# Hybrid decoder layer on one core: modulation blocks in pairs with three projections between their slots, and two half blocks beside q3

## What is computed

```python
mod = jnp.dot(jax.nn.silu(c), w_ada[l]) + b_ada[l]          # 6 vectors of 2048 for each of 9 sequences
sh1, sc1, g1, sh2, sc2, g2 = jnp.split(mod[:, None, :], N_MOD, axis=-1)
h = rmsnorm(x, g_mix[l]) * (1 + sc1) + sh1
z = jnp.dot(h, w_in[l])
zq, zk, zv, zu, gq, gk, gv, gg, ga = jnp.split(z, split_idx, axis=-1)
# window attention on q, k, v; causal pooling on u; gated linear attention (4 heads) on gq, gk, gv, gg, ga
x = x + g1 * jnp.dot(mix, w_out[l])
h2 = rmsnorm(x, g_ffn[l]) * (1 + sc2) + sh2
gate, up = jnp.split(jnp.dot(h2, w_gu[l]), 2, axis=-1)
x = x + g2 * jnp.dot(jax.nn.silu(gate) * up, w_down[l])
```

## Time and profile before

| | |
|---|---|
| median of three runs | 2444.57 us (2444.43 to 2444.83) |
| the profiled execution | 2438.74 us, its span 2436.6 us |
| TensorE busy | 2321.5 us (95%), mean granted clock 0.985 |
| VectorE, ScalarE, GpSimd busy | 1550.0, 922.1, 240.6 us |
| HBM read and written | 365.45 and 54.08 MB, 172 GB/s over the span |
| matmuls of the projections (L1948) | 4704 of 289 to 303 ns each |
| chain that ended last | PE 91%, DMA 3%, DVE 3%, issue 2%, ACT 1% |

### The profile page before, as it was taken

One profiled execution on the slowest core, in us unless ns is written; L12 is line 12 of the kernel. 1 busy time (PEld: TensorE's weight loads), 2 busy tenths in 40 slices (PEclk: granted clock), 3 DMA queues, 4 the chain that ended last, 5 costly groups with the idle time before them and its releaser, 6 DMA issues.

```text
span 2436.6 us, 44374 instructions
## 1 busy us (share of the span) xinstructions
PE 2321.5 (95%) x18645; PEld 2173.4 (89%) x18645; DVE 1550.0 (64%) x2240; ACT 922.1 (38%) x1328; POOL 240.6 (10%) x289
## 2 busy tenths in 40 slices
PE   5689999999999999899999999999999989999996
PEld 1179888888887899899999999999999989999996
DVE  0442642333324322887888888888788878888898
ACT  2122432323233222654444444444444433333443
POOL 3150240000000111100000000000000211011131
PEclk9989999999999999999999999999999999999998
DMA  9955465655563433223433443344344676365552
GB/s 340 345 184 184 155 168 176 226 166 204 176 212 107 173 114 115 109 102 137 169 129 121 159 166 137 137 169 141 124 160 152 260 271 226 132 217 191 181 216 87
DMA packets 191078, 422.43 MB, mean 173 GB/s; under 512 B 14692, under 2 KB 116884, under 8 KB 188832
## 3 DMA queue, kind: packets, MB, share of 16 engines
q1 hardware_dynamic: 171072, 341.35, 40.8%
q0 software_dynamic: 17216, 73.78, 8.6%
q10 hardware_dynamic: 2592, 4.46, 0.5%
HBM read 365.45 MB, written 54.08 MB: 172 GB/s over the span
## 4 chain that ended last, share of the span: by engine, by line
PE 91%; DMA 3%; DVE 3%; issue 2%; ACT 1%; POOL 0%; SPq 0%; DVEq 0%; POOLq 0%; ACTq 0%
PE PJ L2327 28%; PE PS L2327 28%; PE PJ L1948 25%; DMA AR<-in_weights 3%; PE PJ L1901 2%; PE PJ L2292 1%; PE PS L2183 1%; PE PJ L1891 1%; PE PS L2292 1%; PE PJ L2269 1%; PE PJ L1913 1%; DVE X L1868 0%; PE PS L2221 0%; PE PS L2186 0%; DVE HS L1790 0%
## 5 line engine op out<-in xcount | busy, mean ns | idle before, releaser
L2327 PE MATMUL PS<-HS,WO 128*128 128x272 f32 x5376 | 686.3, 289 | 10.8 <-issue 10.1
L2327 PEld LDWEIGHTS PS<-HS,WO 128*128 128x128 f32 x5376 | 681.4, 189 | 12.3 <-issue 12.3
L2327 PE MATMUL PJ<-HS,WO 128*128 128x272 f32 x5376 | 683.0, 289 | 0.0
L2327 PEld LDWEIGHTS PJ<-HS,WO 128*128 128x128 f32 x5376 | 679.7, 188 | 0.0
L1115 ACT ACTIVATE WO<-GR 128x1024 fp32r<-128x1024 f32 (+1 forms) x462 | 477.1, 1033 | 511.7 <-PE PS L2327 246.9
L1643 DVE TENSOR_TENSOR WO<-GR,WO 128x1024 fp32r<-128x1024 f32 (+1 forms) x462 | 555.7, 1203 | 120.4 <-ACT WO L1115 120.2
L1948 PE MATMUL PJ<-HH,WH 128*128 128x272 f32 x1568 | 347.0, 303 | 18.4 <-issue 8.0
L1948 PE MATMUL PJ<-HL,WH 128*128 128x272 f32 x1568 | 327.1, 290 | 0.0
L1948 PE MATMUL PJ<-HH,WL 128*128 128x272 f32 x1568 | 325.5, 289 | 0.0
L1274 DVE TENSOR_TENSOR WL<-RW,WH 128x1024 fp32r<-128x1024 f32 x102 | 130.8, 1286 | 281.5 <-ACT WH L854 281.2
L1948 PEld LDWEIGHTS PJ<-HH,WH 128*128 128x128 f32 x1568 | 247.5, 191 | 52.7 <-issue 41.0
(11 more groups left out here) (310 smaller groups left out, 1871.7 us busy)
## 6 DMA issues: line engine op xcount, KB each, us to landing
GR<-in_weights SPq DMA_DIRECT2D x264, 512.0 KB, 6.8
AR<-in_weights SPq DMA_DIRECT2D x256, 256.0 KB, 4.5
RW<-in_weights SPq DMA_DIRECT2D x102, 512.0 KB, 4.7
HS<-act_parts POOLq DMA_DIRECT2D x91, 544.0 KB, 5.9
act_parts<-SQ SPq DMA_DIRECT2D x40, 952.0 KB, 7.0
AR<-in_weights SPq DMA_DIRECT2D x64, 512.0 KB, 5.3
MIX<-in_xT SPq DMA_DIRECT2D x1, 4352.0 KB, 17.0
X<-in_xT POOLq DMA_DIRECT2D x4, 1088.0 KB, 9.8
```

What stands on the lines that cost most here:

```text
L2327: mm = e.matmul(out, w[part], HS[:, HS_AT[QUARTER[i]], y, (2 * first + k) % (KT // 2), :], start=OPENS[i] and k == 0 and x == 0, stop=k == ...
```

## The change

It does four things.

- The whole blocks are made in the order 0, 4, 1, 5, 2, 6, 3, 7 (`ADA_ORDER`), shift and scale of the same 512 features in turn. They use one pair of banks (`PS` 0 and 1) in place of two, so each block waits for the copy of the one before, and its turn stands behind slot 1 of the next block.
- k, v and q0 (`FIRST_TILES` = 3; q0 in `PS` 2 and 3) are issued by units, k by k: lots of three units stand behind every second slot of blocks 4 to 7 at the places `UNITS_AT`, ten lots for k = 0 to 9; k = 10 and 11 follow the last turn, and k = 12 to 15 come projection by projection. `project_two` isn't used there any more, and v's transposes stand beside q1.
- Tiles 0 to 2 are loaded ahead of block 3, tiles 3 to 5 ahead of block 5, tiles 6 to 8 behind the last slot. The sum over x moves from block 3 to block 2. VectorE's and ScalarE's orders follow.
- The half block that stood beside q0 moves on: q1 has the first, q2 the second, q3 the third and the fourth (behind units 3 and 11, turned behind 7 and 14). u0 and all behind it keep theirs. In SyncE's loop the half blocks start at q1's tile in place of q0's.

```diff
-ROWS = [V_W + n for n in range(4)] + [W_V[n] + x for n in W_TILES[2:] for x in range(2)]
+ROWS = [V_W, V_W + 1, W_V["q0"], V_W + 2, V_W + 3, W_V["q0"] + 1]
+ROWS += [W_V[n] + x for n in W_TILES[3:] for x in range(2)]
...
-SUM_AT = 3
-H_AT = 5
+SUM_AT = 2
+ADA_ORDER = (0, 4, 1, 5, 2, 6, 3, 7)
+FIRST_TILES = 3
+UNITS_AT = ((4, 5), (4, 7), (5, 1), (5, 3), (5, 5), (5, 7), (6, 1), (6, 3), (7, 3), (7, 5))
...
-            if n == ADA_V * (A_FIRST - 1):
-                for t in range(RAW):
-                    load(At(t))
+            if n in (ADA_V * 3, ADA_V * 5):
+                for t in range(FIRST_TILES):
+                    load(At(t + (FIRST_TILES if n > ADA_V * 3 else 0)))
             load_ada(n)
+        for t in range(LEAD):
+            load(At(t + RAW))
         load_half(0)
         x = 0
-        for t in range(T_OUT):
-            if t >= T_W["q0"] and t % 2 == 0 and t != T_W["ga"]:
+        for t in range(LEAD, T_OUT):
+            if t >= T_W["q1"] and t % 2 == 0 and t != T_W["ga"]:
                 x += 1
                 if x < N_HB:
                     load_half(x)
...
+                for n in range(3):
+                    hi(At(n))
+            if b == A_FIRST - 2:
+                for n in range(3, 6):
+                    hi(At(n))
+            rows(b, 0)
+            if b in (3, 4, 6):
+                q = (3, 4, 6).index(b)
+                for k in range(4 * q, 4 * q + 4):
                     h_hi(k)
...
-        def ada_block(b, pair):
-
-            if b >= 2:
-                e.wait_ge(S["ada_rows"], b - 1)
+        def ada_block(b, side):
+
+            if b:
+                e.wait_ge(S["ada_rows"], b)
...
+                for job in side.get(s, ()):
+                    job()
...
+        def first_tiles(t, k):
+
+            if k % 8 == 0:
+                e.wait_ge(S["lo"], FIRST_TILES * (k // 8 + 1))
+                if k == 0:
+                    e.wait_ge(S["rms"], 1)
+            e.wait_ge(S["h_lo"], k + 1)
+            accumulate(At(t), At(FIRST_TILES * (k // 8) + t), k)
+
+        units = [(k, x) for k in range(KT - 4) for x in range(FIRST_TILES)]
 
         for b in range(A_FIRST):
-            ada_block(b, b % 2)
-            if b:
-                turn_rows(b - 1, (b - 1) % 2)
+            side = {1: [lambda b=b: turn_rows(b - 1)]} if b else {}
+            for n, (at, s) in enumerate(UNITS_AT):
+                if at == b:
+                    side.setdefault(s, []).extend(lambda x=x, k=k: first_tiles(x, k) for k, x in units[3 * n:3 * n + 3])
+            ada_block(b, side)
             if b == SUM_AT:
                 sum_x()
-        turn_rows(A_FIRST - 1, (A_FIRST - 1) % 2)
+        turn_rows(A_FIRST - 1)
+        for k, x in units[3 * len(UNITS_AT):]:
+            first_tiles(x, k)
+        for x in range(FIRST_TILES):
+            for k in range(KT - 4, KT):
+                first_tiles(x, k)
...
-        project_two(At(0), At(0), 0, A_FIRST)
-        jobs = {"q0": {4: [v_by_token]}, "ga": {4: [dec_scores], 10: [dec_turn], 13: [dec_values]}}
-        for n, name in enumerate(W_TILES[2:]):
-            m, side = At(M_W[name]), jobs.get(name, {})
-            if name != "ga":
-                side = joined(side, ada_beside(m, A_FIRST + n, 6, 11))
-            project(m, At(T_W[name]), side, A_FIRST + n)
+        jobs = {"q1": {4: [v_by_token]}, "ga": {4: [dec_scores], 10: [dec_turn], 13: [dec_values]}}
+        for n, name in enumerate(W_TILES[3:]):
+            m, b, side = At(M_W[name]), A_FIRST + n, jobs.get(name, {})
+            if name == "q3":
+                side = joined(ada_beside(m, b, 3, 7), {11: [lambda m=m, b=b: half_after(m, b + 1)],
+                                                       14: [lambda m=m, b=b: turn_after(m, b + 1)]})
+            elif name != "ga":
+                side = joined(side, ada_beside(m, b, 6, 11))
+            project(m, At(T_W[name]), side, b + (name == "ga"))
```

More of the change, by code:

```diff
@@ L862, in evacuate, with rows @@
             a.activation(halves(dst), banks(m), func).then_inc(freed[m.mod(2)], 1)
-        def rows(step, pair):
+        def rows(step, bank):
+            src = (PS if step < A_FIRST else PJ)[:, bank, :]
             halves_made = step - A_FIRST + 1
@@ L923, in _ @@
             if name != "ga":
-                rows(A_FIRST + n, (m + 1).mod(2))
-            else:
+                rows(A_FIRST + n, 2 * (m + 1).mod(2))
+            if name == "ga":
                 a.wait_ge(S["dec_shift"], 1)
@@ L932, in _ @@
             hi(v + (1 + LEAD))
+            if name == "q3":
+                rows(A_FIRST + n + 1, 2 * (m + 1).mod(2))
             if name == "ga":
@@ L1317, in _, with h_group, h_los @@
             .then_inc(S["neg_sinks"], 1)
-        def h_group(b):
-            scale_by(b, "g_mix", KT + 4 * (b - 4), 4, 4 * (b - 4))
-            for k in range(4 * (b - 4), 4 * (b - 4) + 4):
+        def h_group(q):
+            scale_by(2 * q + 1, "g_mix", KT + 4 * q, 4, 4 * q)
+            for k in range(4 * q, 4 * q + 4):
                 h_aff(k)
[L1324 to L1340, removed]
-        lo(At(2))
-        for k in range(KT - 4, KT):
-            h_lo(k)
-        for n in range(4):
-            lo(At(n + LEAD))
-        for n, name in enumerate(W_TILES[2:]):
+        def h_los(q):
+            for k in range(4 * q, 4 * q + 4):
+                h_lo(k)
+        for b in range(3):
+            mod_part(b, 1)
+        d.wait_ge(S["rms"], 1)
+        for w in range(2):
+            d.reciprocal(RN0[:, HT * w:HT * w + HT], RN0[:, HT * w:HT * w + HT]).then_inc(S["rstd"], 1)
+        d.wait_ge(S["rstd"], 2)
+        for k in range(4):
+            nrm_x(k)
+        h_group(0)
+        for n in range(3):
+            lo(At(n))
+        for k in range(4, 8):
+            nrm_x(k)
+        h_los(0)
+        mod_part(3, 1)
+        h_group(1)
+        for k in range(8, KT):
+            nrm_x(k)
+        h_los(1)
+        mod_part(4, 1)
+        mod_part(5, 1)
+        h_group(2)
+        for n in range(3, 6):
+            lo(At(n))
+        h_los(2)
+        mod_part(6, 1)
+        mod_part(7, 1)
+        h_group(3)
+        h_los(3)
+        for n in range(6, 9):
+            lo(At(n))
+        for n, name in enumerate(W_TILES[3:]):
             m, v = At(M_W[name]), At(T_W[name])
@@ L1903, in ada_half, with turn_rows @@
                 mm.then_inc(S["ada_used"], 1)
-        def turn_rows(step, pair):
+        def turn_rows(step, pair=None):
             e.wait_ge(S["ada_rows"], step + 1)
-            if step >= 2:
-                e.wait_ge(S["mod_done"], step - 1)
+            if step:
+                e.wait_ge(S["mod_done"], step if step <= A_FIRST else step - 1)
+            out = PS[:, 1, :] if step < A_FIRST else PJ[:, 2 * pair + 1, :]
             made, n = (ADA0, 4) if step < A_FIRST else (ADAR, 2)
             for f in range(n):
-                mm = e.matmul(PJ[:, 2 * pair + 1, NSEQ * f:NSEQ * f + NSEQ], made[:, P * f:P * f + P],
+                mm = e.matmul(out[:, NSEQ * f:NSEQ * f + NSEQ], made[:, P * f:P * f + P],
                               SEL[:, :], start=True, stop=True)
@@ L1942, in accumulate @@
         def accumulate(m, v, k):
-            out = [PJ[:, 2 * m.mod(2) + w, 0:HT] for w in range(2)]
+            out = [bank[:, 0:HT] for bank in
+                   ((PS[:, 2, :], PS[:, 3, :]) if m.base == M_W["q0"] else
+                    (PJ[:, 2 * m.mod(2), :], PJ[:, 2 * m.mod(2) + 1, :]))]
             wh, wl = (t[:, P * (k % 8):P * (k % 8) + P] for t in (WH[v.mod(HIS)], WL[v.mod(RAW)]))
```

62 lines of the change are left out of this document (34 added, 28 removed).

## The result

The changed kernel takes **2537.98 us** (median of 4 runs, 2533.75 to 2546.72), the kernel before beside it 2444.5 (2442.11 to 2444.83). The ratio is 1.0391, 95% interval 1.0364 to 1.0419. The direction was forecast, the size was not: 2537.98 lies 30 us above the range.

The account below looks back on a forecast made before the run. Loads were taken to pace the front, TensorE to bound the kernel from q0 on. Front -28 and half blocks +67 on the profiled 2438.74 gave 2477.7; with 5.83 to the median, 2483.5 us, range 2460 to 2508.

Parts of the forecast that it names:

- Part 1, the front: Front until the slots are done: slots end near 131.5, k, v and q0 at 147.0, clock stays up.
- Part 2, ga's start: From q1 to ga: q1 starts 31.5 us earlier, ga 28.5 less about 0.5; front -28 (24 to 35).
- less about 0.5 if the second half block of q3 waits for its last load: At q3, before ga: deduction from ga's 28.5 us advance, the load being asked for some 8 units earlier.
- Part 3, the half blocks: From u0 through four heads: 28 half blocks lose one projection of load lead; +67 us (41 to 98).
- landing at U + 10.3: Late half blocks: last load lands 10.3 us after U, the projection's start; bounds 9.2 and 11.4.
- stall forecast: Each half block from u0 on: 9.0 us less the time from projection start to half block.
- gq's stall: Heads' gq half block: comes 6.3 us after its projection starts, so it stalls 2.7 us per head.
- upper bound (landing at 11.4): Half blocks from u0 on: +98 us if the last load lands 11.4 us after the projection starts.
- Rival C: Heads' gk, gv1, gg0: stalls bring the clock down, 3 us of slow work each; 29 us more, 2512; chance 0.10.
- Rival A: From u0 on: half blocks land soon enough, stalls sum to 12, front gain stays; 2429 us; chance 0.10.
- D: Front: first units wait for operands and hold the slots; gain near 10, 2501 us; chance 0.02.
- B: Front: every slot costs TensorE its full 0.98 and refills come late; 8 us more, 2491; chance 0.08.

Follow-up runs that it names:

- experiments 1 and 2: First: changed kernel, SyncE issues a half block beside ga too, lead restored, 2415.9 us. Second: kernel before, SyncE also skips q3's projection, lead lost, 2566.54 us.
- experiment 1: Changed kernel with one edit: SyncE issues a half block beside ga's projection too, giving back the lead of one projection; 2415.9 us, ratio 0.9886.
- experiment 3: Changed kernel, late loads kept, with resultless matmuls (fillers) added ahead of slots 1 to 3 of late half blocks: many 2542.7 us, few 2511.33 us.

## Why the prediction was wrong, step by step

**Part 1, the front: right.** Slots done at 131.5 forecast, 130.6 measured, with the last turn at 131.30. k, v and q0 end at 147.0 forecast, 146.1 measured. Clock from 105 to 150 forecast to stay up: 1.00. Other executions of the same front end it between 144.8 and 151.2. By the medians the front is worth 28.2 and 28.6 us (experiments 1 and 2), which is the -28 of the sum.

**Part 2, ga's start: some 4 us off in the trace.** Forecast 194, measured 198.4. The term that failed is "less about 0.5 if the second half block of q3 waits for its last load". I counted the time from the issue to the need as 8 units and did not cost the landing: the last of the eight loads landed 13.8 us after the first was issued (179.4 to 193.2), while GpSimd's stores of the caches ran. With the stores at u0 it is 10.9, and 4.5 us came back in the trace.

**Part 3, the half blocks: the mechanism right, the size little over half.** Forecast +67, measured +126.5 in the profiled executions and 122 by the medians. Two steps failed: the sum put the slower clock behind the stalls at nothing, and it gave all 28 half blocks the same landing at U + 10.3. The timelines split the loss. "Late" is how much later a half block's slots end, counted from the turn of the half block before, than in the kernel of experiment 1; "slow" is how much longer the stretch from there to its own turn is, in which no load is waited for. The last column is "late" with the few fillers of experiment 3. All in us, sums over u0 to u3 or over four heads; gv0's forecast holds the 1.3 of head 0:

| half blocks | stall forecast | late | slow | late, few fillers |
|---|---|---|---|---|
| u0 to u3 | 7.1 | 8.7 | 1.5 | 8.1 |
| gq | 10.8 | 22.2 | 6.9 | 22.1 |
| gk | 16.0 | 24.9 | 7.0 | 27.0 |
| gv0 | 2.1 | 5.6 | 0.0 | 5.1 |
| gv1 | 11.2 | 13.1 | 3.5 | 12.3 |
| gg0 | 17.2 | 19.6 | 12.9 | 17.1 |
| gg1 | 2.4 | 4.3 | 0.0 | 4.3 |
| all | 67 | 98.4 | 31.7 | 96.0 |

98.4 and 31.7 are 130.1. The kernel of experiment 1 is itself 3.2 us shorter behind ga's start than the one before, and 130.1 less 3.2 is the 126.5, to within 0.4.

- *The clock* was put at nothing and is 31.7 us. The stretches of "slow" hold the same matmuls in the same order, and with the few fillers "slow" is 0 everywhere. The fillers' kernel is 26.7 us faster by the medians and 34.4 by the profiled executions.
- *The landing at U + 10.3* was near where GpSimd moves little: 10.3 in head 1's gk, and 9.7 to 11.5 at the others read in the chain. The stalls of gk, gv1 and gg1 in heads 1 to 3 came out near the 4.0, 2.8 and 0.6 of the forecast: in the run with few fillers the slots of head 1 end 4.2, 2.8 and 1.0 later than before.
- *gq's stall* was 2.7 in the sum. Its slots end 6.0 us later in heads 1 and 2 and 7.4 in head 3, but 2.9 in head 0: 11.4 us more than forecast in all. The loads land at U + 13.0 to 14.4 in heads 1 to 3, where GpSimd swaps a head's state of 1 MB out and in at the same time (the software queue moves 2.00 MB from 452 to 467 us), and at U + 10.4 in head 0, where it swaps none. This was to be seen in the trace of before, had I looked at the queues in gq and not only in the stretch of one gg. Moving the swap was not tried, so that it is the cause is argued and not shown.
- *Head 0's gk* is 11.4 us later than before instead of 4.0, another 7. Its last load lands at U + 17.2, beside the stores of the pooling; moving these was not tried either.
- *The rest*, some 13 us, is spread over the other half blocks.

That the sum of "late" equals the 98 which the prediction had as its upper bound (landing at 11.4) is chance: it comes from a few late landings. The range's upper end, 2508, left out this bound of its own, which gives 2519 with the least front.

**Rival C was the case, on top of stalls longer than forecast.** Its chance of 0.10 was too low; its price of 29 us was near the 31.7 measured, in part by luck. Behind the gk, gv1 and gg0 that it named the loss is 23.4 and not 29, and 6.9 stand behind gq, which it left out. The sign named for it, a granted clock below 0.95 between 220 and 800, came true with 0.90. (Its row of the 0.5 clock stands behind a wait of 8.1 us, 125.5 to 133.6, not of 7.) The argument against it was the row of the front, where slots 1.6 apart kept the clock at 1.00. But there TensorE was 37.51 busy of 50.20, three quarters, and in the stall above 1.51 of 4. The row was far from the case, and the same view shows it. It could not be used against C. The Trainium skill (TensorE: Matmul & The Clock Gate, section HAM oscillation) describes this pattern, a wait for DMA ahead of each piece of work that takes the clock back every time; the windows at 482 to 494 us agree, with 0.94, 0.50 and 0.71. Not every stall here does so: behind gv0's and gg1's late slots nothing was lost.

**Rival A** (halves soon enough) fell by its own measure: U + 8.5 was its point, 9.7 and more was measured. By the limit that the Trainium skill gives (DMA: Bandwidth & Descriptors, section Specifications) they would have come at 8.5; the case's rows, which the prediction followed, were nearer. **D** and **B** fell with the front's times. The range was too narrow at its upper end: it didn't hold C, which belonged into the sum as soon as a dozen stalls of 3 to 4 us did.

## What to carry to other kernels

When a loop that issues loads is shifted, count for each load the projection in which it is issued and the one that uses it, before and after; the lead can be lost by a start condition that looks like a mere change of phase. When a forecast contains many waits of TensorE of several us each, price the work behind each wait at the low clock too, and take what the clock does from rows in which the engine did the like. Compare the waits and the delay apart: they are different numbers. Before moving a store out of a crowded stretch, find who waits for its semaphore.

## What the runs showed of the hardware

- Work added to a stalled TensorE can shorten a kernel: 26.7 us less with some 300 matmuls more, as the granted clock stayed at 0.98 instead of 0.90. With nearly twice as many (579) the gain was gone, as they ran past the landing.
- In head 1's gk a stall in which TensorE was 1.51 us busy of 4 was followed by 0.50 and then 0.71; with fillers it was 3.55 and 3.85 of 4, and the clock stayed at 1.00. The slowed work is the work behind the wait, 31.7 us over 28 half blocks.
- Eight loads of 256 KB behind one of 512 KB landed 9.7 to 11.5 us after that one was issued in most half blocks, 13.0 to 14.4 while GpSimd's queue moved some 2 MB, and 17.2 and 19.2 beside the pooling's stores.
- The front's pace varies by some 6 us between executions of kernels whose fronts are alike: q1 at 144.8 to 147.6 in six of them, and at 151.2 in the one whose granted clock from 54 to 106 us was 0.77 (0.93 to 1.00 in the six), with 296 GB/s against 322 to 331. Which of the two came first is not shown.
